# First row tile in two halves, columns of the contraction dealt out anew, and a reordered start and end of the output projection in a one-core encoder layer

## The reference

```
h = rmsnorm(x, norm1_g)
q, k, v, u = split(h @ w_in)              # 512, 128, 128 and 512 columns
q, k = rope(rmsnorm(q)), rope(rmsnorm(k))
a = softmax(q k^T / 8) v                  # 8 query heads, 2 key heads, per sequence
p = pooling of u over windows of 2, 4, 8, 16 tokens, a 128x128 map per group
x = x + concat(a, p) @ w_out
x = x + relu(rmsnorm(x, norm2_g) @ w_up)^2 @ w_down
```

## Time and profile before

| | |
|---|---|
| median of 3 runs | 1469.5 us |
| profiled execution | 1468.74 us, of which the span is 1467.0 us |
| TensorE busy | 1460.4 us |
| VectorE, ScalarE, GpSimd busy | 1049.4, 731.3, 406.0 us |

### The profile page before, as it was taken

The page is one execution under the profiler, slowest core; times in us unless marked ns, Lnnn a source line. Parts: engine busy times, 40 slices in busy tenths (PEclk is TensorE's granted clock), DMA queues, the critical chain, the costliest instruction groups (busy, mean ns, idle before and its releaser), DMA issues.

```text
span 1467.0 us, 23235 instructions
## 1 busy us (share of the span) xinstructions
PE 1460.4 (100%) x7810; PEld 1305.2 (89%) x7810; DVE 1049.4 (72%) x1241; ACT 731.3 (50%) x1255; POOL 406.0 (28%) x372
## 2 busy tenths in 40 slices
PE   9999999999999999999999999999999999999999
PEld 8999988888888889999999999998888888888887
DVE  7766799999868885444544454549887888878875
ACT  6233398898846755454545454546332323333220
POOL 3467587667735510000000000001230220311300
PEclk9999999999999999999999999999999999999999
DMA  8644341111346748433343334347644344343434
GB/s 266 154 116 118 86 127 39 34 25 25 94 156 233 261 189 342 155 119 130 114 159 121 124 114 159 133 179 282 230 156 159 101 157 138 111 152 112 140 94 184
DMA packets 94443, 212.30 MB, mean 145 GB/s; under 512 B 12080, under 2 KB 31408, under 8 KB 94256
## 3 DMA queue, kind: packets, MB, share of 16 engines
q1 hardware_dynamic: 92192, 200.46, 41.3%
q10 hardware_dynamic: 2192, 11.08, 1.8%
HBM read 133.08 MB, written 71.62 MB: 140 GB/s over the span
## 4 chain that ended last, share of the span: by engine, by line
PE 99%; DMA 0%; ACT 0%; DVE 0%; POOL 0%; issue 0%; ACTq 0%; POOLq 0%
PE ps L959 25%; PE ps L960 25%; PE ps L961 24%; PE ps L1235 6%; PE ps L1116 5%; PE ps L1245 3%; PE ps L1095 3%; PE ps L1131 3%; PE ps L1097 3%; PE ps L1132 3%; DMA g1c<-in_g 0%; PE ps L984 0%; PE ps L1022 0%; PE ps L1023 0%; PE ps L1027 0%; PE ps L993 0%
## 5 line engine op out<-in xcount | busy, mean ns | idle before, releaser
L959 PE MATMUL ps<-h,wuhi 128*128 128x384 f32 (+1 forms) x904 | 301.3, 333 | 0.2 <-issue 0.2
L961 PE MATMUL ps<-h,wulo 128*128 128x384 f32 (+1 forms) x904 | 301.1, 333 | 0.0
L960 PE MATMUL ps<-h,wuhi 128*128 128x384 f32 (+1 forms) x904 | 301.1, 333 | 0.0
L959 PE MATMUL ps<-wdhi,hidhi 128*128 128x512 f32 x672 | 261.5, 389 | 0.1
L960 PE MATMUL ps<-wdlo,hidhi 128*128 128x512 f32 x672 | 261.4, 389 | 0.0
L961 PE MATMUL ps<-wdhi,hidlo 128*128 128x512 f32 x672 | 261.4, 389 | 0.0
L2351 DVE TENSOR_TENSOR yacc<-yacc,ps 128x1024 f32<-128x1024 f32 x167 | 203.3, 1217 | 76.6 <-PE ps L961 76.6
L1368 ACT ACTIVATE hidhi<-hin 128x1024 fp32r<-128x1024 f32 (+1 forms) x72 | 86.9, 1207 | 300.7 <-PE ps L961 291.6
L2265 DVE TENSOR_TENSOR u<-u,ps 128x384 f32<-128x384 f32 x96 | 53.1, 553 | 181.5 <-PE ps L961 181.5
L959 PEld LDWEIGHTS ps<-h,wuhi 128*128 128x128 f32 x904 | 169.7, 188 | 0.6 <-issue 0.4
L960 PEld LDWEIGHTS ps<-h,wuhi 128*128 128x128 f32 x904 | 169.7, 188 | 0.0
(11 more groups left out here) (236 smaller groups left out, 2809.3 us busy)
## 6 DMA issues: line engine op xcount, KB each, us to landing
hd<-hout SPq DMA_DIRECT2D x64, 384.0 KB, 3.2
hin<-hd SPq DMA_DIRECT2D x48, 512.0 KB, 3.6
hd<-hout SPq DMA_DIRECT2D x32, 576.0 KB, 2.8
hin<-hd SPq DMA_DIRECT2D x24, 768.0 KB, 4.4
wuraw<-in_w_up SPq DMA_DIRECT2D x17, 1024.0 KB, 6.0
wdraw<-in_w_down SPq DMA_DIRECT2D x8, 2048.0 KB, 9.6
h<-h2d ACTq DMA_DIRECT2D x7, 1536.0 KB, 10.8
x2in<-in_x SPq DMA_DIRECT2D x12, 512.0 KB, 3.4
```

The source lines that it names most:

```text
L959: pe.matmul(out, w_hi, m_hi, start=start, stop=False, skip_group_check=resumed)
L960: pe.matmul(out, w_hi, m_lo, start=False, stop=False, skip_group_check=resumed)
L961: return pe.matmul(out, w_lo, m_hi, start=False, stop=stop, skip_group_check=resumed)
```

## The change

- The 1024 columns are dealt out in two halves: block 4h + j holds columns 512h + 4p + j. So blocks 0 to 3 of a row tile need only its first 512 columns. w_in's rows, g1 and the loads of all row tiles follow. A later tile is loaded by 8 DMAs instead of 4 and turned by two VectorE instructions instead of one.
- Tile 0 is loaded as two halves, with weight rows 0 and 1 between them. TensorE turns blocks 0 to 3 as soon as the first half and the identity are there, and blocks 4 to 7 after the first weight row's products. The order of low(k) on TensorE and of the splits on ScalarE is changed to suit.
- The zeros of the warm-up are 128 columns, read four times, instead of 512.
- `project_out` puts tile 0 in PSUM banks 4 and 5 and drops its wait for a folded block. The first two folded blocks are moved by a DMA of their own, the third by another.
- The last tile's output projection finishes its first 512 columns before the other 512, and VectorE's residual of the first half is moved ahead of the splits before it.
- GpSimd's last attention sum waits until VectorE has split all four other blocks of w_out (`wo_lo`) instead of until GpSimd has rounded them (`wo_hi`).

```diff
-        zeros = at("zeros", X + 11264, [512], F32R)
+        zeros = at("zeros", X + 11264, [P], F32R)
...
+        def out_bank(p):
+            return 2 * (p % 2) if p else 4
...
-            return xin[:, i].rearrange("p (c k) -> p k c", k=KT)[:, k]
+            return xin[:, i].rearrange("p (h c k) -> p h k c", h=2, k=KT // 2)[:, k // 4, k % 4]
...
-            return x[t * P:(t + 1) * P, q * 256:q * 256 + 256].rearrange("(b t) c -> t b c", b=4)
+            return x[t * P:(t + 1) * P].rearrange("(b t) (h q c) -> h q t b c", b=4, h=2, q=4)[h, q]
...
-        w_rows = w_in.rearrange("(p k) n -> k p n", k=KT)
+        w_rows = w_in.rearrange("(h p k) n -> h k p n", h=2, k=KT // 2)
...
                 for q in range(4):
-                    sp.dma_start(quarter_in(t % 2, q), quarter_of(t, q)).then_inc(x_in[t % 2], 16)
+                    for h in range(2):
+                        sp.dma_start(quarter_in(t % 2, q, h), quarter_of(t, q, h)).then_inc(x_in[t % 2], 16)
...
-            sp.dma_start(xin[:, 0], x[0:P]).then_inc(x_in[0], 16)
-            for k in range(5):
+            sp.dma_start(xin[:, 0, 0:512], x[0:P, 0:512]).then_inc(first_in, 16)
+            load_wi(0)
+            load_wi(1)
+            sp.dma_start(xin[:, 0, 512:D], x[0:P, 512:D]).then_inc(x_in[0], 16)
+            for k in range(2, 5):
                 load_wi(k)
...
+                    sp.wait_ge(wf_lo, 2)
+                    sp.dma_start(wolo[:, 0:2].bitcast(F32), wqlo[:, 0:2].bitcast(F32)).then_inc(wf_moved, 16)
                     sp.wait_ge(wf_lo, 3)
-                    sp.dma_start(wolo[:, 0:3].bitcast(F32), wqlo[:, 0:3].bitcast(F32)).then_inc(wf_moved, 16)
+                    sp.dma_start(wolo[:, 2:3].bitcast(F32), wqlo[:, 2:3].bitcast(F32)).then_inc(wf_moved, 16)
...
+            def turn_first(h):
+
+                k0, k1, out = first_part(h)
+                for k in range(k0, k1):
+                    mm = pe.transpose(out[:, k - k0], row_in(0, k), ident[:])
+                mm.then_inc(xT_done if h == 2 else xT_half, 1)
...
                 for k in range(KT):
+                    if k == 1:
+                        pe.wait_ge(x_in[0], 16)
+                        turn_first(2)
+                        low(0)
                     if k == 5:
+                        low(4)
                         pe.wait_ge(x_in[1], 16)
...
-                    if k:
-                        low(k - 1)
+                    if k == 1 or k in (3, 4) or k > 5:
+                        low(k if k == 1 else k - 1)
...
-                pe.wait_ge(x_in[0], 16)
-                for h in range(3):
-                    k0, k1, out = first_part(h)
-                    for k in range(k0, k1):
-                        mm = pe.transpose(out[:, k - k0], row_in(0, k), ident[:])
-                    mm.then_inc(xT_done if h == 2 else xT_half, 1)
+                turn_first(0)
+                turn_first(1)
...
-            pe.wait_ge(ident_in, 16)
+            pe.wait_ge(first_in, 2 * 16)
...
-                if p < 2:
-                    pe.wait_ge(wf_lo, p + 3)
-                else:
+                if p == 1:
+                    pe.wait_ge(wf_lo, 4)
+                elif p:
                     pe.wait_ge(x2_done, p - 1)
...
+            def project_last():
+
+                p, i = TT - 1, (TT - 1) % 2
+                pe.wait_ge(c_lo, TT)
+                pe.wait_ge(x2_done, p - 1)
+                for h in range(2):
+                    bank, cols = out_bank(p) + h, slice(h * 512, h * 512 + 512)
+                    for n, (c, w) in enumerate(((chi, wohi), (clo, wohi), (chi, wolo))):
+                        if (h, n) == (1, 1):
+                            transpose_x2(p - 1)
+                        for j, k in enumerate(SLOT_ROWS):
+                            mm = pe.matmul(ps[:, bank], c[i][:, k], w[:, j, cols], start=(n == 0 and j == 0),
+                                           stop=(n == 2 and j == KT - 1))
+                    mm.then_inc(out_done, 1)
...
-            act.dma_start(g1c[:], g1.rearrange("(p k) -> p k", k=KT)).then_inc(g1_in, 16)
+            act.dma_start(g1c[:].rearrange("p (h k) -> p h k", h=2), g1.rearrange("(h p k) -> p h k", h=2, k=KT // 2)).then_inc(g1_in, 16)
...
             split_first(0)
+            split_first(1)
             act.wait_ge(g1_in, 16)
             split_wi(0)
-            split_first(1)
             split_wi(1)
             split_first(2)
...
             split_wi(4)
+            split_wi(5)
             square_x(0)
-            for k in range(5, KT):
+            for k in range(6, KT):
...
-                dve.transpose(blocks_out(), blocks_in(t % 2)).then_inc(xT_done, 1)
+                dve.transpose(blocks_out(0), blocks_in(t % 2, 0))
+                dve.transpose(blocks_out(1), blocks_in(t % 2, 1)).then_inc(xT_done, 1)
...
                 else:
+                    residual_left()
                     lo_h2(p - 1)
-                    lo_wu(0, 2)
-                    residual_last()
-                    for o in (3, 5, 6):
+                    residual_right()
+                    for o in (2, 3, 5, 6):
                         lo_wu(0, o)
                     scale_last()
...
                 if n == OUTS - 1:
-                    pool.wait_ge(wo_hi, 4)
+                    pool.wait_ge(wo_lo, 4)
```

More of the change, by code:

```diff
@@ L208, in hybrid_layer @@
         psw = ps[:].rearrange("p b c -> p (b c)")
-        ident_in = sem("ident_in")
+        first_in = sem("first_in")
         g1_in = sem("g1_in")
@@ L604, in row_in, with quarter_in, quarter_of, blocks_in @@
         def row_in(i, k):
-            return xin[:, i].rearrange("p (c k) -> p k c", k=KT)[:, k]
-        def quarter_in(i, q):
-            return xin[q * 32:q * 32 + 32, i].rearrange("t (b c) -> t b c", b=4)
-        def quarter_of(t, q):
-            return x[t * P:(t + 1) * P, q * 256:q * 256 + 256].rearrange("(b t) c -> t b c", b=4)
[L614 to L618, removed]
+            return xin[:, i].rearrange("p (h c k) -> p h k c", h=2, k=KT // 2)[:, k // 4, k % 4]
+        def quarter_in(i, q, h):
+            return xin[q * 32:q * 32 + 32, i].rearrange("t (b h c) -> t b h c", b=4, h=2)[:, :, h]
+        def quarter_of(t, q, h):
+            return x[t * P:(t + 1) * P].rearrange("(b t) (h q c) -> h q t b c", b=4, h=2, q=4)[h, q]
+        def blocks_in(i, h):
+            return xin[:, i].rearrange("p (b h c k) -> p h k b c", b=4, h=2, k=KT // 2)[:, h]
+        def blocks_out(h):
+            return xT[:, h * 4:h * 4 + 4].rearrange("p k (b t) -> p k b t", b=4)
         def stat_area():
@@ L1195, in warm @@
                 for _ in range(n):
-                    pe.matmul(ps[:, 4], zeros[:, 0:P], zeros[:], start=True, stop=True)
+                    pe.matmul(ps[:, 4].rearrange("p (k c) -> p k c", c=P), zeros[:], zeros[:].unsqueeze(1).to_broadcast([P, 4, P]),
+                              start=True, stop=True)
             pe.wait_ge(mexp_set, 1)
             warm(6)
-            pe.wait_ge(ident_in, 16)
+            pe.wait_ge(first_in, 2 * 16)
             first_block()
@@ L1336, in down_chunk @@
                         down_product(n, z, u, o, last)
-            for p in range(TT):
+            def project_last():
[11 more added lines that the diff above has]
+                    mm.then_inc(out_done, 1)
+            for p in range(TT - 1):
                 project_out(p)
+            project_last()
             up_product(0, 0, 1, 0, 0)
@@ L1373, in square_x @@
                     act.wait_ge(x_in[t], 16)
+                    act.wait_ge(first_in, 2 * 16)
                 else:
@@ L1691, in load_h2 @@
                 if o == 0:
-                    act.wait_ge(out_done, TT)
+                    act.wait_ge(out_done, TT + 1)
                     for q in range(QT_TILES):
@@ L2153, in residual_last, with residual_right @@
                 dve.tensor_tensor(x2in[:, 1, 0:512], x2in[:, 1, 0:512], psw[:, 1024:1536], ALU.add).then_inc(x2_half, 1)
+            def residual_right():
+                dve.wait_ge(out_done, TT + 1)
                 dve.tensor_tensor(x2in[:, 1, 512:D], x2in[:, 1, 512:D], psw[:, 1536:2048], ALU.add).then_inc(x2_done, 1)
```

22 lines of the change are left out of this document (11 added, 11 removed).

## The result

| | before | after |
|---|---|---|
| median, us (22 runs each) | 1469.01 (1468.62 to 1471.01) | 1472.13 (1470.78 to 1473.18) |
| ratio after to before | | 1.0018, 95% interval 1.0013 to 1.0024 |
| profiled execution, us (span) | 1468.74 (1467.0) | 1470.78 (1469.0) |

What follows compares the result with a forecast made beforehand. TensorE was taken as the bound, busy 1460.4 of 1467.0 us. Start +0.5, output projection's start -0.5 and end -0.3 sum to -0.3 us: 1468.4 for the profiled execution, 1469.2 as median, range 1467.7 to 1471.2.

Steps and rivals of the forecast that it cites:

- Start: +0.5, bounds -0.35 and +0.9: Kernel's start: the next block begins at 17.3 instead of 16.77, 0.5 us later, as g1 lands late and transposes move.
- g1 ... 6.15: Start: g1's doubled pieces each wait for one packet of SP's queue, so g1 lands at 6.15, 0.46 us later.
- Four transposes ... some 0.45: Start: four of tile 0's eight transposes move behind the first weight row, adding some 0.45 us to TensorE's path.
- Rival 2: Start: TensorE's longer stand lets its clock fall, products run at half rate, +1.7 us, 1470.9 us; chance 0.08.
- a new wait over 0.5 us between 17 and 400 us: Sign that the prediction is wrong: TensorE shows a new wait over 0.5 us between 17 and 400 us.
- Output projection's start -0.5: Output projection's start: tile 0 no longer waits for the third folded block; -0.5 us, bounds -0.6 and +0.1.
- rival 4: Middle and end: the removed waits were covered anyway, only the start's +0.5 stays, 1470.0 us; chance 0.14.
- Its end -0.3: Output projection's end: the first half's residual sum leaves the path; gain 0.3 us, bounds -0.5 and +0.3.
- Later row tiles 0: Later row tiles: doubled loads push VectorE by up to 6.1 us, within 9.2 us of cover; cost 0.
- GpSimd's sum at 0: Output projection's start: GpSimd's last sum waits for VectorE's splits but ends before TensorE wants it; cost 0.
- Rival 3: Later row tiles: SP's queue is the bound, TensorE waits at the pooling columns, +6 us, 1475 us; chance 0.04.
- Rival 1: Start: g1 is not late, its extra pieces go in one turn; sum -1.15 us, 1468.4 us; chance 0.2.

Runs made afterwards that it cites:

- e1: The kernel before with the start's edits alone (first tile's halves, dealt-out columns, later tiles in eight loads, ScalarE's new order): 1472.06 us, ratio 1.0017.
- e5: The changed kernel with ScalarE's squares of the first row tile moved back ahead of weight row 5: 1471.80 us, ratio 1.0016 against before.
- e6: The changed kernel with GpSimd's last split of a query weight block waiting for VectorE's low part of the pooling maps: 1470.36 us, ratio 1.0007 against before.
- e7: The changed kernel with both edits, squares ahead of weight row 5 and GpSimd's last split behind the maps: 1470.01 us, ratio 1.0006 against before.
- e2: The kernel before with the output projection's start alone (the middle part): 1468.40 us, ratio 0.9990.
- e3: The kernel before with the output projection's end alone: 1469.64 us, ratio 1.0000.
- e4: The changed kernel without its start, that is middle and end parts on the kernel before: 1469.29 us, ratio 1.0001 against before.
- e8: The kernel before with the middle part alone and GpSimd's last split behind the maps: 1469.50 us, ratio 0.9999.
- e11: The kernel before with g1 loaded in 256 pieces of 16 bytes instead of 128 of 32: 1471.85 us, ratio 1.0012.
- e10: The e7 kernel with three more warm-up products in TensorE's stand before the first weight product: 1469.12 us, ratio 0.9995 against before.
- e16: The changed kernel without its end part, with squares early, GpSimd's last split behind the maps and three products in the stand: 1469.06 us, ratio 0.9995 against before.
- e17: The changed kernel with three more warm-up products in TensorE's stand before the first weight product, nothing else: 1472.05 us, ratio 1.0014 against before.
- e18: The changed kernel with squares early and three products in the stand, without GpSimd's wait: 1471.35 us, ratio 1.0010 against before.
- e14: The kernel before with twelve idle transposes ahead of second_qkv and GpSimd's last split held behind the maps: 1471.96 us, ratio 1.0021.
- e13: The kernel before with twelve idle transposes (1.3 us in all) between the first block and second_qkv: 1472.15 us, ratio 1.0016.
- e15: The kernel before with the middle part, GpSimd's last split behind the maps and two more warm-up products in TensorE's stand: 1469.09 us, ratio 0.9995.
- e12: The kernel before with the first tile loaded as two column halves back to back, 256 pieces of 2 KB instead of 128 of 4 KB: 1472.87 us, ratio 1.0024.

## Why the prediction was wrong

In the profile of after the forecast's -0.3 us became +2.0. The start cost 0.8 more than forecast, the first fold, which stands nowhere in the sum, cost 1.6, the end gave 0.3 less, and the output projection's start gave 0.3 more.

- **"Start: +0.5, bounds -0.35 and +0.9" is the term that failed by size.** It measured +1.3 in the profile of after, and +1.3 on the mean of the next block's start (18.4 in the five profiles of the changed start without products, after, e1, e5, e6 and e7; 17.1 in the five with before's start, before, e2, e3, e4 and e8). Its cause was wrong too. "g1 ... 6.15" did not happen: g1 landed at 5.43, in e11 at 5.81. Left out were ScalarE's squares, which the diff moves behind weight row 5 and which I did not price, and the later weight rows: the last of the eight lands 0.5 us later in after. The squares were in the diff to be read. In e10, with the clock up and the squares early, 0.4 us of the start's loss is left (17.19 against 16.77), and the last weight row lands 0.4 later there.
- **"Four transposes ... some 0.45" held** as work (0.39 from 7.46 to 7.85), but not what it leaves: a stand of 1.4 to 1.6 us before the first product (0.75 before), which they used to fill.
- **Rival 2 (chance 0.08) happened**, in a part of the runs. It had the place and the loss right: TensorE's products run at half pace in four of the five profiles of the changed start without products, in e1, e6 and e7 with 0.50 between 8 or 9 and 11 us, in e5 from the first product to 9.9. It had the moment wrong: in e1, e6 and e7 the clock was still up when the products began and fell some 1.5 us later. A mean clock below 1.000 stands against 23 of 66 runs of that start (the changed kernel, e1, e5, e6, e7), against none of 44 with products in the stand (e10, e16, e17, e18) and against 7 of 151 of the kernel before. That count is not a measure of the loss: half pace as in e5 and e11 goes with a mean of 1.000, and within e6 and e7 the runs below 1.000 are not the slower ones (medians 1469.6 against 1470.6, and 1469.9 against 1470.5). The rival's price was too high: 0.9 us of the median (e10 against e7) rather than 1.7. ScalarE's late rows cover part of it.
- **The first fold is in no term and no rival.** I had read TensorE's own waits only, and wrote that work on other engines costs nothing until TensorE waits for it. The row that mattered was one of VectorE's, the 1.16 us low part of the maps: 0.68 is what it takes undisturbed (e6), so it was already waiting for GpSimd. The Trainium skill has the rule, which I did not look up: page "SBUF — State Buffer", section "Who interferes with whom", says that a VectorE instruction with two inputs in SBUF contends with a GpSimd instruction that reads SBUF, and that the port pair they share is an exclusive lock. The trace agrees: 0.68 us alone, 2.75 when it comes 0.18 us behind GpSimd's change to a split of 2.38, while low parts that read PSUM take 0.69 beside the same splits. In the changed kernel this is worth 1.8 to 2.2 us by the medians (e6 against the changed kernel, e7 against e5, e10 against e18): the largest term of all. By the prediction's own signs it was wrong here: a new wait over 0.5 us between 17 and 400 us is one that it names.
- **"Output projection's start -0.5" had the right place and was too small**: 0.76 us by the steps, in every profile that has the middle part, beyond the bound of -0.6. The low part lost nothing any more (3.79), where the forecast left 0.1, and the first product's step and the high part gave 0.44 instead of 0.32. It is also the only part whose interval lies below 1 by itself (e2). So rival 4, by which mid and end give nothing, is out for the middle.
- **"Its end -0.3" is not seen in the time** (e3: 1.0000). In e3's profile TensorE loses 0.2 us up to 540, where the early residual half pushes two splits, gains 0.4 between 540 and 550 and has lost 0.3 of it again by 570, at a stand of the kind described under e14; in after the gain of 0.2 is lost by 570 in the same way.
- **"Later row tiles 0" and GpSimd's sum at 0 held.** Rival 3 is out: VectorE's longer wait never reached TensorE, which is 1.30 us late at the next block and 1.27 at 385. Rival 1 had g1 right, and the result wrong: twice the pieces put g1 1.07 (e11) and 1.26 us (after) behind the identity instead of 1.04, not 2.1, so the rule quoted for that rival fits and the prediction's reading of the 1.05 us does not.

The account for the median, each kernel against the runs of the kernel before beside it: as changed +3.1, with products in the stand (e17) +2.4, with the squares early too (e18) +1.7, with GpSimd's turn settled too (e10) -0.4. The last step is clear of the scatter. The first is not: the two medians themselves, 1472.13 and 1472.05, are 0.1 apart. What is left open is the 1.3 us by which a pure delay costs more than itself (e13, e14). Of the versions tried only the middle part alone was faster than the kernel before by its interval (0.9981 to 0.9999), by less than the 0.2% that the prediction says can be told, and e4, e8 and e15, which contain it, do not repeat it.

## What to carry to other kernels

Where TensorE is busy all the time, look at the other engines' instructions that take longer than their like: VectorE's 1.16 us for a 0.68 us split was a collision that happened to end in time, and 0.7 us of shift between the two engines turned it into a stand of 1.6 us. Order such a pair by a wait on the engine with slack, and a later change no longer meets it by chance. When work is taken out of a stand ahead of the first products, put idle products in its place, and check that nothing moved on a side engine (here one line of squares) stands between the last loads and the last products: here neither helped without the other. And before a stand or a gain in one profile is believed, set each product's start against that of the same product before: the shift then shows where time is lost, and where it comes back.

## What the hardware showed that I had not expected

- VectorE's split of two operands in SBUF and GpSimd's splits exclude one another by whole instructions. Begun 0.6 or 0.4 us ahead of GpSimd's change from one split to the next, VectorE's took 1.16 or 0.96 us and GpSimd's second 2.86 or 2.85 (before, e13). Begun 0.18 us behind the change, VectorE's took 2.75 and GpSimd's 2.38 (after).
- Pieces of 2 KB instead of 4 KB in one 512 KB load, with one issue more (0.45 us), put off the landing of the eight weight rows behind it by 1.4 us at first and 0.9 in the end (e12). Doubling g1's 128 pieces put off g1 by 0.1 (e11).
- TensorE kept the 1.2 GHz level from the warm-up up to 10.7 us in e11, where it had hardly stood (0.39 and 0.16 us), and left it by 5.4 in before with a longer stand to come. Which of the two a run takes could not be told from its rows. The column PEclk shows 1.00 in both; only the steps tell them apart (0.64 us from pair to pair of products against 0.35).
